# Delta rule of a two-block layer stack: next pair prepared between the levels, both norms in the neighbouring chains

## What is computed

```python
qkv = jax.nn.silu(_causal_conv(qkv_b, conv_w))          # 3 x 1024 features: q, k, v of 8 heads of 128
q = _l2norm(q) * (dk ** -0.5); k = _l2norm(k)
a_low = jnp.where(strict, bc[..., :, None] * kk * decay_mat, 0.0)
sol = lax.linalg.triangular_solve(eye + a_low, [v * beta, k * beta * exp(gcum)], ...)
attn = einsum(q, k) * decay_mat; qe = q * exp(gcum); kd = k * exp(gcum_end - gcum)
# per chunk:  v_new = u - w @ S;  o = qe @ S + attn @ v_new;  S = S * g_end + kd^T @ v_new
hb = _head_rmsnorm(hb, g_gdn_norm) * silu(zb)
y = sigmoid(gate_a) * (ha @ w_branch_a) + sigmoid(gate_b) * (hb @ w_branch_b)
```

## Time and profile before

| | us |
|---|---|
| median of 3 runs (lowest, highest) | 4223.08 (4221.22, 4227.52) |
| the profiled execution, its own time | 4219.93 |
| its span | 4218.1 |
| TensorE busy | 3825.1 (91%) |
| VectorE busy | 1864.5 (44%) |
| ScalarE busy | 1233.0 (29%) |
| GpSimd busy | 213.5 (5%) |

### The profile page before, as it was taken

How to read it: one execution, slowest core, us unless ns; L and a number is a source line. 1 busy time by engine, 2 the same in 40 slices (tenths; PEclk the granted TensorE clock), 3 DMA queues, 4 the chain that set the end, 5 groups by cost and what they waited for, 6 DMA issues and landing times. The chain is left out here.

```text
span 4218.1 us, 52826 instructions
## 1 busy us (share of the span) xinstructions
PE 3825.1 (91%) x20657; PEld 3163.3 (75%) x20657; DVE 1864.5 (44%) x2517; ACT 1233.0 (29%) x1819; POOL 213.5 (5%) x266
## 2 busy tenths in 40 slices
PE   7787999988999798998888989979899888898997
PEld 6655999985888586785886768858678588676885
DVE  3365524335534225275444443342526544444333
ACT  2144212224322134223323232223422332323122
POOL 0000000000000000001330000000000133000000
PEclk9888999978999899997999999989999799999998
DMA  2100222211222121220002222212122000222222
GB/s 104 47 20 31 90 91 90 81 52 37 90 100 100 64 80 50 90 80 21 0 0 84 81 80 95 93 63 80 50 90 80 21 1 0 79 86 80 95 93 81
DMA packets 50851, 279.59 MB, mean 66 GB/s; under 512 B 11677, under 2 KB 14757, under 8 KB 21445
## 3 DMA queue, kind: packets, MB, share of 16 engines
q1 hardware_dynamic: 50682, 277.26, 19.3%
HBM read 274.94 MB, written 2.27 MB: 66 GB/s over the span
## 5 line engine op out<-in xcount | busy, mean ns | idle before, releaser
L334 PE MATMUL ps<-xs,ffn_w 128*128 128x512 f32 x2112 | 482.8, 391 | 29.7 <-DVE xs L597 29.7
L334 PEld LDWEIGHTS ps<-xs,ffn_w 128*128 128x128 f32 x2112 | 398.7, 189 | 114.3 <-issue 31.3
L334 PE MATMUL ps<-u,mlp_w 128*128 128x264 f32 (+1 forms) x2880 | 456.2, 321 | 14.8 <-DVE mlp_w L591 10.0
L334 PEld LDWEIGHTS ps<-u,mlp_w 128*128 128x128 f32 x2880 | 417.2, 190 | 53.4 <-issue 15.5
L334 PE MATMUL ps<-hn,mlp_w 128*128 128x264 f32 (+1 forms) x2304 | 363.7, 320 | 0.0
L334 PEld LDWEIGHTS ps<-hn,mlp_w 128*128 128x128 f32 x2304 | 332.4, 188 | 30.4 <-issue 0.5
L334 PE MATMUL ps<-xs,cv_w 128*128 128x512 f32 x1152 | 273.5, 400 | 8.5 <-DVE cv_w L591 8.5
L334 PEld LDWEIGHTS ps<-xs,cv_w 128*128 128x128 f32 x1152 | 219.0, 190 | 63.0 <-issue 9.3
L334 PE MATMUL ps<-ff,ffn_w 128*128 128x512 f32 x1056 | 240.0, 389 | 0.0
L381 ACT CAST ffn_w<-raw 128x2048 fp32r<-128x2048 f32 (+1 forms) x74 | 124.1, 1677 | 383.1 <-PE ps L334 343.1
L334 PEld LDWEIGHTS ps<-ff,ffn_w 128*128 128x128 f32 x1056 | 198.2, 188 | 41.1
(11 more groups left out here) (412 smaller groups left out, 5382.5 us busy)
## 6 DMA issues: line engine op xcount, KB each, us to landing
raw<-in_w_ffn_up SPq DMA_DIRECT2D x44, 1024.0 KB, 4.9
raw<-in_w_up SPq DMA_DIRECT2D x32, 1024.0 KB, 4.9
raw<-in_w_down SPq DMA_DIRECT2D x32, 1024.0 KB, 4.9
raw<-in_w_conv SPq DMA_DIRECT2D x24, 1024.0 KB, 4.9
raw<-in_w_ffn_down SPq DMA_DIRECT2D x32, 704.0 KB, 4.1
raw<-in_w_mqk SPq DMA_DIRECT2D x10, 1024.0 KB, 4.9
raw<-in_w_mv SPq DMA_DIRECT2D x8, 1024.0 KB, 4.8
raw<-in_w_mo SPq DMA_DIRECT2D x8, 1024.0 KB, 4.9
```

Of the source, the lines that this page charges most:

```text
L334: ins = nc.tensor.matmul(bank(u)[:, h, :], w[:, s, wp, k * g.bw + j * P:k * g.bw + (j + 1) * P], g.xs[:, xp, k, h * n:(h + 1) * n], start= ...
```

## The change

1. `cv` becomes three chained products, in the order keys, queries, values. Beside it `HeadRows` squares the 16 tiles of k and q on ScalarE and sums them over partitions by 16 matmuls with `pick`, two after each of blocks 1 to 8. Of k the reciprocal root becomes a row; q is not normalised at all: its sum goes, with the epsilon, into `acc`, the start of the sum that the last norm uses. The gate rows are split into high and low parts there.
2. The stages "qkn2", `spread_rows` and "gn" are gone, and with them `g_rows_b` and the copies of q, k and v. `delta_rule` spreads each row by two fp32r matmuls into PSUM where it is needed, and works in place in `qkv`.
3. `delta_rule` is written out, without the loop. Pair 0 is prepared first, in seven steps; the seven steps of pair i+1 stand between the levels of pair i, for one head before the products w and z, for the other behind them. All of them use bank 3, so the recurrence of a pair waits for the last step of the next (`vb_done`). The first y is a transpose now. The squares of the output are taken on ScalarE and summed by TensorE in the next pair's level 0, and added to `acc` by VectorE.
4. Beside `branch_b`, `HeadNorm` makes the reciprocal root of `acc`, spreads 8 rows by 16 matmuls after blocks 0, 1 and 2, and scales two tiles of `hb` ahead of each of the first four evacuations. `hb` now lies at the right end of SBUF.

```diff
--- before.py
+++ after.py
...
+class HeadRows(Beside):
...
+    def tensor(self, pe, n):
+        if 1 <= n <= 8:
+            for t in (2 * n - 2, 2 * n - 1):
+                pe.wait_ge(self.s["squared"], t + 1)
+                self.nc.tensor.matmul(self.ps[0:GH, 1 + 2 * (t // GH), :], self.pick[:, t % GH, :], self.sq[:, t % 4, :], start=(t % GH == 0),
+                                      stop=(t % GH == GH - 1)).then_inc(self.s["picked"], 1)
+    def scalar(self, act, n):
+        nc, s = self.nc, self.s
+        if n == 0:
+            for r in range(2):
+                nc.scalar.copy(self.rows[:, 2 - r, 0, :], self.g_rows[:, r, :]).then_inc(s["high_done"], 1)
+        if 0 <= n < 8:
+            g = self.products[n // 4]
+            for t in (2 * n, 2 * n + 1):
+                act.wait_ge(g.s["half_done"], 2 + t % GH + 1)
+                if t >= 4:
+                    act.wait_ge(s["picked"], t - 3)
+                nc.scalar.activation(self.sq[:, t % 4, :], g.dst[:, t % GH, :], ACT.Square).then_inc(s["squared"], 1)
+        if n == 5:
+            act.wait_ge(s["eps_set"], 1)
+            act.wait_ge(s["picked"], GH)
+            nc.scalar.activation(self.acc, self.ps[0:GH, 1, :], ACT.Sqrt, bias=self.small[:, 0:1]).then_inc(s["rooted"], 1)
+        if n == 7:
+            act.wait_ge(s["inverted"], 1)
+            nc.scalar.copy(self.rows[:, 0, 0, :], self.acc).then_inc(s["inv_high"], 1)
+    def vector(self, dve, n):
+        nc, s = self.nc, self.s
...
+        if n == 6:
+            dve.wait_ge(s["rooted"], 1)
+            nc.vector.reciprocal(self.acc, self.acc).then_inc(s["inverted"], 1)
...
+        if n == 9:
+            dve.wait_ge(s["picked"], 2 * GH)
+            dve.wait_ge(s["low_done"], 3)
+            nc.vector.tensor_scalar(self.acc, self.ps[0:GH, 3, :], EPS * GDK * GDK, None, ALU.mult).then_inc(s["summed"], 1)
...
+class HeadNorm(Beside):
...
+    def tensor(self, pe, n):
+        if n in (0, 1, 2):
+            pe.wait_ge(self.s["low_done"], 1)
+            for h in ((0, 1, 2, 3), (4, 5), (6, 7))[n]:
+                if n:
+                    pe.wait_ge(self.s["scaled"], h - 3)
+                for e in range(2):
+                    ins = self.nc.tensor.matmul(self.ps[:, 2 * (h % 4) + 1, :], self.sel[:, h, :], self.rows[:, 0, e, :], start=(e == 0), stop=(e == 1))
+                ins.then_inc(self.s["spread"], 1)
+    def scalar(self, act, n):
+        nc, s = self.nc, self.s
+        if n == -1:
+            act.wait_ge(s["eps_set"], 1)
+            nc.scalar.activation(self.acc, self.acc, ACT.Sqrt, bias=self.small[:, 0:1], scale=1.0 / GDK).then_inc(s["rooted"], 1)
+            act.wait_ge(s["inverted"], 1)
+            nc.scalar.copy(self.rows[:, 0, 0, :], self.acc).then_inc(s["high_done"], 1)
...
+    def ahead(self, dve, n):
+        nc, s = self.nc, self.s
+        if n < GH // 2:
+            for h in (2 * n, 2 * n + 1):
+                dve.wait_ge(s["spread"], h + 1)
+                nc.vector.scalar_tensor_tensor(self.out[:, h, :], self.out[:, h, :], self.gain, self.ps[:, 2 * (h % 4) + 1, :],
+                                               ALU.mult, ALU.mult).then_inc(s["scaled"], 1)
+            dve.wait_ge(s["scaled"], 2 * n + 2)
...
+                def spread(e, s, i, r):
+                    for part in range(2):
+                        ins = nc.tensor.matmul(ps[:, 4 * e + 3, :], sel[:, 2 * i + e, :], rows[:, r, part, :], start=(part == 0), stop=(part == 1))
+                    ins.then_inc(s["spread"], 1)
...
+                def prepare(i, n, e, f, s):
+
+                    if n == 0:
+                        if i == 1:
+                            pe.wait_ge(s["vb_done"], 1)
+                        if i >= 2:
+                            pe.wait_ge(added, 2 * (i - 2) + e + 1)
+                        spread(e, s, i, 0)
+                    if n == 1:
+                        pe.wait_ge(s["khat_done"], i + 1)
+                        spread(e, s, i, 1)
+                    if n == 2:
+                        pe.wait_ge(s["kb_done"], i + 1)
+                        spread(e, s, i, 2)
+                    if n == 3:
+                        pe.wait_ge(s["arg_done"], i + 1)
+                        pe.wait_ge(s["eg_done"], i + 1)
+                        each(e, 3, tile_of(1, i, e), f["kb"], s["kk_done"])
+                    if n == 4:
+                        pe.wait_ge(s["n_done"], i + 1)
+                        each(e, 3, tile_of(1, i, e), tile_of(0, i, e), s["qk_done"])
+                    if n == 5:
+                        pe.wait_ge(s["att_done"], i + 1)
+                        turn(e, 3, tile_of(1, i, e), s["turned_k"])
+                    if n == 6:
+                        pe.wait_ge(s["kd_done"], i + 1)
+                        pe.wait_ge(s["kbe_done"], i + 1)
+                        turn(e, 3, tile_of(2, i, e), s["turned_v"])
...
+                def pick_squares(i, e, f, s):
+                    pe.wait_ge(s["squared"], i + 1)
+                    pe.wait_ge(s["o_copied"], i + 1)
+                    nc.tensor.matmul(ps[0:GH, 4 * e + 3, :], pick[:, 2 * i + e, :], f["sq"][:, :], start=True, stop=True).then_inc(s["picked"], 1)
...
+                        if i and b == 0:
+                            for e, f, s in both:
+                                pick_squares(i - 1, e, f, s)
+                        if i + 1 < pairs:
+                            prepare(i + 1, b, *both[0])
+                        if b:
+                            for e, f, s in both:
+                                pe.wait_ge(s["y_copied"], (levels - 1) * i + b)
+                                pe.wait_ge(s["u_done"], levels * i + b)
+                                each(e, 2, f["y"], f["u"], s["w_filled"])
+                                if b < levels - 1:
+                                    each(e, 1, f["u"], f["y"], s["z_filled"])
+                        if i + 1 < pairs:
+                            prepare(i + 1, b, *both[1])
...
+                            if c == 0:
+                                pe.wait_ge(s["vb_done"], min(i + 2, pairs))
...
+                        if i + 1 < pairs and b in (2, 3):
+                            decays(i + 1, *both[b - 2])
...
+                        nc.scalar.copy(out[:, 2 * i + e, :], ps[:, 4 * e + 3, :]).then_inc(s["o_copied"], 1)
+                        if i:
+                            act.wait_ge(s["picked"], i)
+                        nc.scalar.activation(f["sq"][:, :], ps[:, 4 * e + 3, :], ACT.Square).then_inc(s["squared"], 1)
...
+                def prepared(i, n, e, f, s):
+                    h, d = 2 * i + e, i % 2
+                    if n == 0:
+                        dve.wait_ge(s["spread"], 3 * i + 1)
+                        nc.vector.tensor_tensor(tile_of(1, i, e), tile_of(1, i, e), bank(e, 3), ALU.mult).then_inc(s["khat_done"], 1)
+                    if n == 1:
+                        dve.wait_ge(s["spread"], 3 * i + 2)
+                        dve.wait_ge(s["khat_done"], i + 1)
+                        nc.vector.tensor_tensor(f["kb"][:, :, :], tile_of(1, i, e), bank(e, 3), ALU.mult).then_inc(s["kb_done"], 1)
+                    if n == 2:
+                        dve.wait_ge(s["spread"], 3 * i + 3)
+                        nc.vector.tensor_tensor(f["dm"][d][:, :, :], bank(e, 3), mask4, ALU.add).then_inc(s["arg_done"], 1)
+                    if n == 3:
                         dve.wait_ge(s["kk_done"], i + 1)
                         dve.wait_ge(s["dm_done"], i + 1)
+                        nc.vector.tensor_tensor(f["big_n"][d][:, :, :], bank(e, 3), f["dm"][d][:, :, :], ALU.mult).then_inc(s["n_done"], 1)
+                    if n == 4:
+                        dve.wait_ge(s["qk_done"], i + 1)
+                        dve.wait_ge(s["n_done"], i + 1)
+                        nc.vector.tensor_tensor(f["att"][d][:, :, :], bank(e, 3), f["dm"][d][:, :, :], ALU.mult).then_inc(s["att_done"], 1)
+                        nc.vector.tensor_tensor(tile_of(0, i, e), tile_of(0, i, e), f["eg"][d][:, :, :], ALU.mult).then_inc(s["qe_done"], 1)
+                    if n == 5:
                         dve.wait_ge(s["turned_k"], i + 1)
+                        dve.wait_ge(s["qe_done"], i + 1)
+                        nc.vector.tensor_tensor(f["kd"][d][:, :, :], bank(e, 3), wide(KD, h), ALU.mult).then_inc(s["kd_done"], 1)
+                        nc.vector.tensor_tensor(tile_of(1, i, e), bank(e, 3), wide(BETA_E, h), ALU.mult).then_inc(s["kbe_done"], 1)
+                    if n == 6:
                         dve.wait_ge(s["turned_v"], i + 1)
...
+                def add_squares(i, e, f, s):
+                    dve.wait_ge(s["picked"], i + 1)
+                    if 2 * i + e:
+                        dve.wait_ge(added, 2 * i + e)
+                    nc.vector.tensor_tensor(acc, acc, ps[0:GH, 4 * e + 3, :], ALU.add).then_inc(added, 1)
+
+                for n in range(levels):
+                    for e, f, s in both:
```

(27 more changed lines are left out.)

276 lines of the change are left out of this document (118 added, 158 removed).

## The result

The changed kernel takes 4102.97 us (median of four runs, 4097.80 to 4107.24), the kernel before 4224.07 in the same comparison: a ratio of 0.9714 (95% interval 0.9697 to 0.9730), 121 us less. 4085 was forecast, -138. The profiled execution took 4099.06 against 4219.93.

What follows compares the result with a forecast made beforehand. TensorE's queue was taken to set the levels, other engines' round trips the rest. Per layer 241.2 for 328.0, plus 13.7, 3.6 and 0.5, gave 259.0: -69.0, or -138 in all, from 4223.1 to 4085 us; range 4060 to 4124.

Steps and rivals of the forecast that it cites:

- End: From the delta rule's last product to `branch_b`: 9.7 us per layer instead of 29.35.
- stage changes: From the end of `cv` to the delta rule's first matmul: only a stage change remains, 5.6 us, formerly 58.5.
- last pair: Levels and recurrence of the delta rule's last pair, with no preparation between them: 40.7 us.
- The average of 60.6: Old delta rule: each pair after pair 0 adds 60.6 us on average, 19 to 20 of it preparation with waits.
- Preparation between the levels: Pairs 1 to 3, inside the previous pair's levels: TensorE is the bound, +7.1 us per pair, 47.8 instead of 40.7.
- Taken as 0: Delta rule levels: added waits of TensorE and VectorE cost nothing; TensorE's were each signalled a level earlier.
- Pair 0: Preparation before pair 0's first level product: 22 us, between 20 at full clock and 24 at half; old 17.6.
- with preparation to follow: Between pairs, last product to next first level product: 7.1 us, bounds 3.5 and 10; 5.6 for the last pair.
- Rival B: Everything thin runs at half clock, in pair 0, borders and `branch_b`: about +13 us per layer, 4111; chance 0.12.
- Sums in the chain: Convolution chain `cv`: 16 added products for the squares at 0.86 us each on TensorE, +13.7 per layer.
- The ring of 11.56: VectorE and ScalarE loop per `cv` block: 11.56 us, 12.64 with two squares, still below TensorE's 12.95.
- `branch_b`: Last norm at the start of `branch_b`: 16 spreads cost +3.6 us per layer, thin cover +0.5, up to 3.

Runs made afterwards that it cites:

- e2: The changed kernel with the delta rule's row spreads using all 128 rows of the array, zero beyond the eighth; 4076.6 us.
- e1: The changed kernel with the sums of squares between pairs in PSUM bank 2, so the next spreads no longer wait for VectorE's addition; 4091.7 us.
- e4: The changed kernel with the squares beside the convolution chain rounded to fp32r and summed by fp32r products; 4075.7 us.
- e10: The changed kernel with squares and sums of k and q and k's inverse root as a stage of its own behind the convolution chain; 4098.9 us.
- e5: The changed kernel with one more VectorE operation of 128x512, result unused, in each of the 48 levels that subtract; 4109.4 us.
- e6: The changed kernel with the edits of e1, e2 and e4 together, full rows also for the last norm's spreads and fp32r squares in the delta rule; 4047.2 us.
- e7: The kernel of e6 with products that nobody reads put where TensorE stands idle around stage changes; 4045.1 us.
- e3: The changed kernel with the next pair's seven preparation steps behind a pair's last level instead of between its levels, on all engines; 4148.3 us.
- e9: The changed kernel with the whole last norm taken out of the chain of `branch_b` and made a stage of its own ahead of it; 4123.9 us.

## Why the prediction was right, and where it was off

The number lies in the range (4060 to 4124), 18 above the forecast; the sign and the mechanism were right. Point by point:

- *End, stage changes, last pair.* 8.4 for 9.7, 5.4 for 5.6, 40.7 for 40.7. Right, and the 9.7 is a slip: its terms 2.4, 1.8, 2.5 and 2.1 add up to 8.8.
- *The sign in the old trace.* Before, the last pair took 42.6, because the clock fell at its start: four products w started 1.71 before the next group, as against 0.90 in the earlier trace rows. The average of 60.6 in the forecast had hidden that. The clock also fell right behind the wait of 3.81 in the preparation of the second pair, and of the third. Both could be read from the old trace and were not (stretches of the kernel before, columns as in the earlier trace rows):

```profile
2042.00:2046.00 4.00, 4.00 (x26) 4.00 (x25) 2.52 (x6) 1.28 (x4) 1.28 (x1) 0.63 0.00 0
...
2168.00:2176.00 8.00, 6.67 (x35) 6.48 (x34) 2.97 (x6) 1.17 (x2) 4.21 (x3) 0.58 0.00 0
```

- *Preparation between the levels.* At full clock a period was 54.7, forecast 54.9, but by two errors against each other. A level of 5.64 holds a hidden wait: the eight products y take 2.07 before, and 1.79 where a step of the preparation stands ahead of them (2047.44 - 2045.66 = 1.78 in the changed kernel). The spreads cost more than their 0.454, by the change between 8 rows and 128 (e2). The third period took 51.8 at full clock (e1, e4, e10), 1.6 less than the 53.4 of the forecast. "Taken as 0" for the added waits was right (43.51 busy of 44), and e5 shows room for another operation.
- *Pair 0.* 22 was taken from walking the steps, between 20 at full clock and 24 at half; the runs gave 26.1 and 24.1, and 22.2 in e2. What failed is the upper bound by the clock. The list behind the 24 has only pair 0's own steps; six spread products of pair 1 and eight products y also stand ahead of pair 0's first w, and took 6.9 in layer 1 (1953.02 to 1959.88) at 0.50.
- *Clock behind the borders.* The step that failed is 7.1 "with preparation to follow". Its TensorE part was priced at full clock throughout. Behind three of four such borders it fell to the 1.2 GHz level: about 3 us each, 9 of the 18 that the forecast missed. The low clock of pair 0 in layer 1 reached 2.0 into the first period, which no term had. Rival B had this mechanism, but with +1.5 a border. Its 4111 is nearer to 4103 than the forecast's 4085, so it deserved more than 0.12.
- *Sums in the chain.* +13.7 was forecast, +16.0 and +16.5 measured: mis-sized was the 0.86, which comes from a stage with nothing but such sums; among fp32r products it is 1.00 (e4). The ring of 11.56 was read rightly in the old kernel, where TensorE needs 11.25 for a block and the ring has no pause in it: low part 2.2, two tiles of convolution 6.9, SiLU 0.5, high part 1.9. But it was carried over to a kernel in which it is shorter. A tile of convolution takes 3.01 in e4 (1838.03 to 1841.05) and took 3.34 before, here the timeline of VectorE of the kernel before:

```profile
1823.37 0.74 DVE L565 TENSOR_SCALAR cv_tmp<-ps,par 128x512 f32<-128x512 f32 x1
...
1826.71 0.74 DVE L565 TENSOR_SCALAR cv_tmp<-ps,par 128x512 f32<-128x512 f32 x1
```

  The hardware loop of `cv` is gone in the changed kernel, which may be why; no run tests it. So the ring is 10.81 and with two squares 11.85 (e4), and it hid what the forecast said, with more room.
- *`branch_b`.* +4.9 and +5.0, forecast 4.1: eight spreads took 2.06 instead of 1.82, and the blocks with four took 12.23, 1.35 more than the 10.88 without, instead of 0.91. It is the same change of rows: with full rows (e6) they took 11.84. No stall of VectorE's. The low clock at its start cost next to nothing (e7), but a second fall behind it cost 2.6 in e3.
- *The low end of the range.* Its terms (pair 0 at 17.6, borders at 5.6, 5.6 and 4.5) take 8.5 per layer off, not 12, and give 4068, not 4061.

In sum, per layer over the forecast: chain +2.4 and +2.9, pair 0 +4.1 and +2.1, periods +6.8 and +1.5, the rest about -1. The +6.8 are two falls behind borders (6.3), the end of pair 0's low clock (2.0) and a second wait longer by 0.35, less 2.0 by which the periods at full clock were forecast too long; the +1.5 are one fall and that wait, less the same 2.0. That the whole came so near is in part luck: these errors stand against each other.

What made the gain is tested only in part: interleaving 40 to 45 of the 121 (e3), the last norm beside `branch_b` 21 (e9), the first norm's place about 0 to 7 (e10). The remaining 50 or so lie in what is no longer done (the norm of q, the copies, the spread rows' stage, a second reciprocal); that was argued from the pieces of the table and not undone by itself.

Open: what exactly lets the clock fall. In five kernels with the wait and the 8-row spreads (the changed one, e4, e5, e9, e10) it fell behind 13 of 20 such borders; with the wait taken away (e1) behind none of 4, with full rows (e2) behind none of 4, with both (e6, e7) behind none of 8, with full rows and a wait of 2.79 behind 3 of 4. So taking away either of the two was enough here, and a longer pause did without the thin spreads; it looks as if they add to each other. Neither decides it alone: the same instructions with the same wait lost the clock in one layer and kept it in the other. Four borders of one execution are few. Whether the 8-column sums count like the 8-row spreads was not tried.
